# Attention heads issued in pairs on TensorE: scores on two row halves, values on two column halves

## The reference, cut to what matters

```python
# even: 8 heads without mask, then 8 with a band mask and a sink
s = jnp.einsum('bqkgd,bskd->bkgqs', qi, k) * scale
p = jax.nn.softmax(s, axis=-1)
o = jnp.einsum('bkgqs,bskd->bqkgd', p, v)
# odd: 16 heads, a bias and a mask of neighbours on every head
s = s + bias
# second, on 16 more keys (meta tokens): 4 differential heads, each of two
# score maps of head size 32, that share one sum of values
attn = p[:, 0] - lam * p[:, 1]
# then 6 heads of size 64 with bias and sink, and 6 of size 96 with a causal mask
return jnp.concatenate([y_a, y_b, y_c], axis=-1) @ w_out
```

## Time and profile before

| what | us |
|---|---|
| median of 3 runs | 1443.31 (1442.8 to 1445.22) |
| profiled execution, span | 1446.3 |
| PE busy | 1368.4 (95%) |
| DVE busy | 990.8 (69%) |
| ACT busy | 755.3 (52%) |
| attention of "even", T(0) to the last V | 42.6 |
| attention of "odd", the same | 42.4 |
| attention of "second", the same | 73.0 |

### The profile page before, as it was taken

One profiled execution on the slowest core, in us unless ns is written; L12 is line 12 of the kernel. 1 busy time (PEld: TensorE's weight loads), 2 busy tenths in 40 slices (PEclk: granted clock), 3 DMA queues, 4 the chain that ended last, 5 costly groups with the idle time before them and its releaser, 6 DMA issues.

```text
span 1446.3 us, 20981 instructions
## 1 busy us (share of the span) xinstructions
PE 1368.4 (95%) x6835; PEld 1116.1 (77%) x6835; DVE 990.8 (69%) x1772; ACT 755.3 (52%) x1324; POOL 113.4 (8%) x150
## 2 busy tenths in 40 slices
PE   4999999899999989999999989999969899999997
PEld 4888877567888878888787568888867665788886
DVE  4877778657777777777745657777754555587775
ACT  4555555555555555555545645555543545455553
POOL 4100003001000010000001310000021110100000
PEclk9999999999999999999999999999989859999999
DMA  9766656525666647666465438666534120376660
GB/s 272 230 189 189 188 146 201 146 88 154 195 189 186 191 138 212 188 189 189 151 198 162 116 89 243 184 186 195 165 120 144 31 75 17 116 217 188 189 189 29
DMA packets 274382, 234.41 MB, mean 162 GB/s; under 512 B 8414, under 2 KB 242526, under 8 KB 274208
## 3 DMA queue, kind: packets, MB, share of 16 engines
q1 hardware_dynamic: 270304, 221.05, 51.7%
q0 software_dynamic: 3744, 12.17, 3.0%
q10 hardware_dynamic: 288, 0.59, 0.1%
HBM read 232.70 MB, written 5.69 MB: 165 GB/s over the span
## 4 chain that ended last, share of the span: by engine, by line
PE 89%; DVE 6%; ACT 2%; issue 2%; POOL 1%; DMA 1%; SPq 0%; POOLq 0%; DVEq 0%; ACTq 0%
PE gu L1377 43%; PE y L1389 25%; PE gu L1448 8%; PE gu L1514 4%; PE y L1557 4%; PE y L1527 2%; DVE sb_w_lo L908 1%; PE y L1550 1%; DVE sb_act_t L954 1%; PE gu L1344 1%; DMA sb_w_raw<-in_ffn_w_gate 1%; PE y L1456 1%; DVE sb_work L932 1%; DVE sb_mwork L1121 0%; ACT sb_prob L755 0%
## 5 line engine op out<-in xcount | busy, mean ns | idle before, releaser
L1377 PE MATMUL gu<-sb_act_t,sb_w_hi 128*128 128x512 f32 x1760 | 622.8, 397 | 5.6 <-DVE sb_act_t L954 5.6
L908 DVE TENSOR_TENSOR sb_w_lo<-sb_w_raw,sb_w_hi 128x1024 fp32r<-128x1024 f32 (+1 forms) x406 | 495.2, 1222 | 157.7 <-ACT sb_w_hi L643 151.2
L643 ACT ACTIVATE sb_w_hi<-sb_w_raw 128x1024 fp32r<-128x1024 f32 (+1 forms) x406 | 426.3, 1052 | 156.5 <-PE y L1389 78.0
L1377 PE MATMUL gu<-sb_act_t,sb_w_lo 128*128 128x256 f32 x1760 | 458.8, 281 | 0.0
L1377 PEld LDWEIGHTS gu<-sb_act_t,sb_w_hi 128*128 128x128 f32 x1760 | 324.5, 189 | 69.8 <-issue 7.0
L1377 PEld LDWEIGHTS gu<-sb_act_t,sb_w_lo 128*128 128x128 f32 x1760 | 333.8, 190 | 19.5
L1389 PE MATMUL y<-sb_w_hi,sb_hid_t 128*128 128x512 f32 x880 | 258.3, 395 | 8.0 <-issue 7.7
L679 ACT ACTIVATE sb_work<-gu 128x256 f32<-128x256 f32 x220 | 84.4, 384 | 281.6 <-PE gu L1377 281.0
L1389 PEld LDWEIGHTS y<-sb_w_hi,sb_hid_t 128*128 128x128 f32 x880 | 165.8, 189 | 44.3 <-issue 9.1
L964 DVE TENSOR_TENSOR sb_work<-gu,sb_work 128x256 f32<-128x256 f32 x220 | 93.2, 424 | 142.4 <-ACT sb_work L679 120.3
L1448 PE MATMUL gu<-sb_w_hi,sb_act_t 128*128 128x512 f32 (+2 forms) x416 | 136.6, 397 | 2.7 <-DVE sb_meta_t L958 2.0
(11 more groups left out here) (168 smaller groups left out, 1126.9 us busy)
## 6 DMA issues: line engine op xcount, KB each, us to landing
sb_w_raw<-in_ffn_w_gate SPq DMA_DIRECT2D x88, 512.0 KB, 3.9
sb_w_raw<-in_ffn_w_up SPq DMA_DIRECT2D x88, 512.0 KB, 3.9
sb_w_raw<-in_ffn_w_down SPq DMA_DIRECT2D x88, 512.0 KB, 3.9
sb_w_raw<-in_odd_w_qkv SPq DMA_DIRECT2D x24, 512.0 KB, 3.9
sb_w_raw<-in_w_gate SPq DMA_DIRECT2D x22, 512.0 KB, 3.9
sb_w_raw<-in_w_up SPq DMA_DIRECT2D x22, 512.0 KB, 3.9
sb_w_raw<-in_w_down SPq DMA_DIRECT2D x22, 512.0 KB, 4.0
sb_w_raw<-in_even_w_in SPq DMA_DIRECT2D x12, 512.0 KB, 3.8
```

The lines of the kernel that those rows point to most:

```text
L643: nc.scalar.activation(w_hi[:, slot, 0:w], w_raw[:, slot, 0:w], ACT.Copy).then_inc(hi_done, 1)
L908: nc.vector.tensor_tensor(w_lo[:, slot, 0:w], w_raw[:, slot, 0:w], w_hi[:, slot, 0:w].bitcast(F32), ALU.subtract).then_inc(lo_done, 1)
L1377: ins = nc.tensor.matmul(gu[:, b, w, 0:width], part[:, s, cols], act_t[:, k, 0:width], start=(k == 0 and i == 0), stop=(k == KT - 1 and i ...
```

## The change

`unit_scores` becomes `pair_scores`: it takes two units, waits for what both need, and issues their matmuls in turns, a query half of the one and then of the other. `values` is split: `diff_values` is as before for a differential head, and `pair_values` takes two heads, waits for the copies of both, and issues their chunks in turns. The loop in `attention` also places them differently: S was issued ahead of T(i) in every step; a pair's S is now issued in every second step, behind T(i) and behind the values.

```diff
+            def pair_scores(pair):
+                for un in pair:
+                    if un.u >= 2:
+                        pe.wait_ge(max_ready, un.u - 1)
+                        before = ALL_UNITS[un.u - 2]
+                        if before.bias is None and not before.mask:
+                            pe.wait_ge(exp_ready, un.u - 1)
                 for t in range(TT):
-                    w = width_of(un)
-                    ins = nc.tensor.matmul(gu[:, b, t, 0:w], qt[rows, un.q, t * P:(t + 1) * P], kt[rows, un.k, 0:w],
-                                           start=True, stop=True)
-                ins.then_inc(scores_ready, 1)
+                    for un in pair:
+                        rows, w = slice(un.base, un.base + un.rows), width_of(un)
+                        ins = nc.tensor.matmul(gu[:, un.u % 2, t, 0:w], qt[rows, un.q, t * P:(t + 1) * P], kt[rows, un.k, 0:w],
+                                               start=True, stop=True)
+                        if t == TT - 1:
+                            ins.then_inc(scores_ready, 1)
...
+            def pair_values(pair):
+                for un in pair:
+                    pe.wait_ge(probs_t_ready, un.t + 1)
+                    bank_ready(un)
+                chunks = 2 if width_of(pair[0]) == SEQ else 3
+                for c in range(chunks):
+                    n = P if c < 2 else META
+                    for un in pair:
+                        half = un.out[1]
+                        ins = nc.tensor.matmul(y[HD * half:HD * half + HD, 2 + out_bank(un), 0:SEQ], values_of(un, c),
                                                prob_t[0:n, un.t % 2, c * SEQ:(c + 1) * SEQ], start=(c == 0), stop=(c == chunks - 1))
-                ins.then_inc(pv_done, 1)
+                        if c == chunks - 1:
+                            ins.then_inc(pv_done, 1)
...
-                turned = None
+                turned = []
                 for i, un in enumerate(units):
-                    if i + 2 < len(units):
-                        unit_scores(units[i + 2])
                     if i == 0:
                         pe.wait_ge(job_copied, jobs)
                     if un.t is not None:
                         turn_probs(un)
-                        if turned:
-                            values(turned)
-                        turned = un
-                    elif turned:
-                        values(turned)
-                        turned = None
+                    if turned and turned[0].diff:
+                        diff_values(turned[0])
+                        turned = []
+                    elif len(turned) == 2:
+                        pair_values(turned)
+                        turned = []
+                    if i % 2 == 0 and i + 2 < len(units):
+                        pair_scores(units[i + 2:i + 4])
+                    if un.t is not None:
+                        turned.append(un)
...
-                values(turned)
+                pair_values(turned)
...
-                    unit_scores(units[0])
-                    unit_scores(units[1])
+                    pair_scores(units[0:2])
```

More of the change, by code:

```diff
@@ L1500, in latent @@
                 ins.then_inc(latent_made, 1)
[L1502 to L1511, removed]
-                for t in range(TT):
-                    w = width_of(un)
-                    ins = nc.tensor.matmul(gu[:, b, t, 0:w], qt[rows, un.q, t * P:(t + 1) * P], kt[rows, un.k, 0:w],
-                                           start=True, stop=True)
-                ins.then_inc(scores_ready, 1)
+            def pair_scores(pair):
[5 more added lines that the diff above has]
+                            pe.wait_ge(exp_ready, un.u - 1)
+                for t in range(TT):
+                    for un in pair:
[4 more added lines that the diff above has]
+                            ins.then_inc(scores_ready, 1)
             def turn_probs(un):
@@ L1536, in values_of, with bank_ready, diff_values @@
                 return work[:, c, c0:c0 + HD] if c < 2 else mwork[0:META, m0:m0 + HD]
-            def values(un):
+            def bank_ready(un):
+                for s_, v_ in bank_waits[un.t]:
+                    pe.wait_ge(s_, v_)
+            def diff_values(un):
                 pe.wait_ge(probs_t_ready, un.t + 1)
[L1540 to L1555, removed]
-                        n = P if c < 2 else META
-                        ins = nc.tensor.matmul(y[HD * half:HD * half + HD, bank, 0:SEQ], values_of(un, c),
@@ new lines, in diff_values @@
+                bank_ready(un)
+                for t in range(TT):
+                    for c in range(3):
+                        n = P if c < 2 else META
+                        ins = nc.tensor.matmul(y[:, 2 + out_bank(un), t * HD:(t + 1) * HD],
+                                               prob_t[0:n, un.t % 2, c * SEQ + t * P:c * SEQ + (t + 1) * P],
+                                               values_of(un, c), start=(c == 0), stop=(c == 2))
+                ins.then_inc(pv_done, 1)
```

## The result

| | before | after |
|---|---|---|
| median | 1444.26 us (4 runs) | 1516.65 us (4 runs, 1514.84 to 1519.54) |
| ratio of the times | | 1.0497, 95% interval 1.0478 to 1.0517 |
| span of the profiled execution | 1446.3 | 1515.4, +69.1 |
| "even": attention, then its output projection | 42.6 + 23.0 | 62.5 + 24.9 |
| "odd" | 42.4 + 23.0 | 64.0 + 25.7 |

A forecast was written before the change was run, and what follows sets the result against it. PE was taken to bound the attention stages. 1446.3 + 25.7 (new order) + 26 (lower clock) + 3 (output projections) = 1501.0 us in the profiled execution, 3.0 above the median, so 1498 was forecast; range 1462 to 1524.

The forecast's parts named there:

- both halves overlap: S and V of a pair: two side by side take the time of one; 2.05 us of PE work saved per pair.
- the loop closes: Attention stages: S now waits behind T and V, which wait for DVE; masked pair 7.15 us against 5.30.
- the clock sinks: Attention stages: PE works 49% of a period, so its clock falls to 1.2 GHz for parts; +26 us.
- the three terms: Whole kernel: +25.7 us for the new order, +26 for the lower clock, +3 for starts of output projections.
- the sum: Three stages at the old clock: extra time of the new order, 8.3 + 8.0 + 9.4 = +25.7 us.
- no wait between scores(4), normalise(3) and scores(5): Sign in the new trace: DVE runs these unbroken, then waits about 3 us for PE in every pair.
- I take 60%: Clock term: chosen share between bounds of 0 and 44 us for the lower clock in the stages, giving +26.
- +3 assumed: Starts of the three output projections may run at the lower clock: half of 6.6 us, three times, by 60%.
- 36 to 64%: Three stages of the kernel before: the busy share that the prediction read for DVE and ACT.
- The clock stays: Rival: PE keeps 2.4 GHz in the stages, so only the new order costs; 1469 us, chance 0.15.
- Other engines the bound: Rival: DVE and ACT become the bound in the stages and the kernel is faster; 1402 us, chance 0.04.
- No overlap: Rival: the heads of a pair don't overlap where they should; +45, 1543 us, chance 0.05.

The follow-up runs named there:

- e9: The changed kernel with useless matmuls filling PE's waits in all three stages, in the bank of the next values: 1473.91 us, ratio 1.0187.
- e5: The changed kernel with paired scores issued ahead of the even unit's transposes and values issued unit by unit: 1432.6 us, ratio 0.992.
- e2: The changed kernel without turns: within a pair, all matmuls of the first unit, then all of the second: 1524.69 us, ratio 1.0597.
- e8: The kernel before the change with 4 useless matmuls in the wait before the first transposes of "second": 1449.34 us, ratio 1.0034.
- e7: The e5 kernel with useless matmuls before the transposes of the differential heads of "second": 1428.53 us, ratio 0.9885.

## Why the prediction was right

The mechanism held: both halves overlap, the loop closes as described, and the clock sinks for PE's waits. But 54.7 us were forecast and 72.4 measured in the medians (69.1 in the profiled span), and each of the three terms was too small.

**The loop: periods right, sum too small.** Predicted 7.15 us for a masked pair at full clock and 9.44 at the lower one; measured 6.97 (e9) and 9.26. Heads without a mask: 6.07 predicted, 5.89 measured at full clock. A pair of differential heads at the lower clock: 10.2 predicted, 10.28 and 9.85 measured between blocks of transposes. The stages with the fill took 49.5, 53.7 and 79.1 us against 50.9, 50.4 and 82.4 in the sum, and +24.5 in all against +25.7. That this comes so close is in part luck, since the sum was made for the clock of the kernel before. At that clock the loop costs 31.4: +8.4 in "even" (8.3 predicted), +11.3 in "odd" (8.0) and +11.7 in "second" (9.4). In "odd" two of five periods at full clock were 0.7 us longer than the 6.63 of the sum (7.39 and 7.28, between starts of S in e9), and in each a row of DVE took 0.8 to 0.9 us more than elsewhere (L1206 1.55 instead of 0.61, L1189 1.00 instead of 0.17) while POOL's L592 ran. That DVE would have no wait between scores(4), normalise(3) and scores(5), and PE one of about 2 and one of about 1.7 us, is about what the timeline shows (2.04 and 1.28).

**The overlap.** 1.13 us for two S and 1.08 for two V. The Trainium skill's rule on weight loads of one row group ("TensorE: Matmul & The Clock Gate", Part 3), by which the two V would not overlap, is not borne out by this trace: two V with the same 128 rows, weight loads included, take the time of one. That S and V of one pair could need turns was right only for the 16 rows.

**The clock: right in direction, mis-sized.** The step that was too small is "I take 60%" of 44, +26. It measured 32.3, which is 73% of the bound (39.2 less the 6.9 that the kernel before lost as well). By time the clock was low for 62, 74 and 80% of the three stages (from 0.69, 0.63 and 0.60), but that is not the right weight: in the pair shown, S at 302.92 still ran in 1.13 us, T at 308.29 took 1.12, V 1.97 and the next S 2.07. In this pair the level fell after PE's waits, and the block of work behind them paid for it. The projections: +3 assumed, +6.0 measured, each up to 2.7 longer. 31.4 + 32.3 + 6.0 = 69.7 us, and the span grew by 69.1.

**A misreading that changed nothing.** In the three stages DVE and ACT were busy for 49 to 64%, not for "36 to 64%": 36% is POOL's share in "odd".

**The rivals.** "The clock stays" was priced at 1469; the kernel in which it was mostly made to stay ran in 1474. "Other engines the bound", 1402, needs a loop that doesn't bind. e5 shows which order comes near: its stages save 18 of the 41 us. That emptying PSUM may become the bound once the matmuls are packed, as the Trainium skill has it ("TensorEngine Tiling (Array Packing)", PSUM Bottleneck), no run here shows: in e5 PE is still the busiest engine, with 4.32 of 4.74 us in a masked pair and 60.2 of 62.8 in "second". "No overlap" was wrong, but for 96 rows, as the prediction had it.

## What to carry to other kernels

Packing small matmuls into row or column halves makes PE's work shorter, but in a pipeline of several engines the first question is where in PE's queue the packed work stands: it must be issued before the instruction that waits for the engine it feeds. Grouping two units also groups what they wait for and what they free; here grouping the scores paid (0.992) and grouping the values did not (1.0068). Count an idle TensorE twice, once as the wait and once as the lower clock on the work behind it, which here cost as much again, 32 of 64 us in the stages.

## What the runs showed of the hardware that was not expected

- Useless matmuls in PE's waits made a kernel 1.5% faster (1494.13 against 1516.65 us), and 2.8% with three stages filled (1473.91).
- Column halves overlap without turns too, as the row halves of S already did: in "even" of e2, where V of one unit is issued whole behind the other's, one V pair at full clock is 8 matmuls in 1.09 us:

```profile
275.96 1.09 PE L1564 MATMUL y<-sb_prob_t,sb_work 128*64 128x256 f32 x8
```

- A chunk of 16 rows between chunks of 128 undoes that: 3.2 instead of 1.7 us. S in 96 rows doesn't overlap at all, 8 matmuls in 2.10 us:

```profile
1275.97 2.10 PE L1515 MATMUL gu<-sb_kt,sb_qt 96*128 96x272 f32 x8
```

- The granted clock fell to 0.50 by 1149.5 us in e8 although PE had been busy without a gap since 1140. What PE did then were transposes of 128 columns, scores in 32 rows, four useless matmuls and values of 64 moving columns. Whether any of it matters was not tried; in e7 and e9 the same kinds ran at 2.4 GHz for parts of the stretch.
